# Index score products of the sparse attention tied to the gate tiles of the merge, which move up in the fill

## The reference, cut to what matters

```
r, k, v, wd, ad, g = split(pa)                  # RWKV: 8 heads of 64, state scanned over time
q, k, v, gate, iq, ik, iw = split(pb)           # DSA: 8 heads; iq has 8 index heads of 64, ik one
# per block of 128 queries:
sc = einsum('bqhd,bsd->bqhs', iq, ik) * 64**-0.5
idx_score = einsum('bqhs,bqh->bqs', relu(sc), iw)     # masked by chunk
sel = top_k(idx_score, 128)                            # keys each query may see
p = softmax(q.k over sel) ; y_b = p.v * sigmoid(gate)
# merge with two gates of 1024 columns each
merged = sigmoid(gm[:, :1024]) * (y_a @ w_a_out) + sigmoid(gm[:, 1024:]) * (y_b @ w_b_out)
x = x + ada_gate * (merged @ w_o)
```

## Time and profile before

| what | value |
|---|---|
| median of three runs | 3110.51 us |
| the profiled execution, its own time | 3113.39 us |
| its span, first to last instruction | 3111.6 us |
| TensorE busy | 2990.5 us, 96% |
| VectorE busy | 1606.2 us, 52% |
| mean granted TensorE clock | 0.983 |

### The profile page before, as it was taken

How to read it: one execution, slowest core, us unless ns; L and a number is a source line. 1 busy time by engine, 2 the same in 40 slices (tenths; PEclk the granted TensorE clock), 3 DMA queues, 4 the chain that set the end, 5 groups by cost and what they waited for, 6 DMA issues and landing times.

```text
span 3111.6 us, 42487 instructions
## 1 busy us (share of the span) xinstructions
PE 2990.5 (96%) x16912; PEld 2391.9 (77%) x16912; DVE 1606.2 (52%) x3295; ACT 1079.1 (35%) x1781; POOL 1412.3 (45%) x1817
## 2 busy tenths in 40 slices
PE   6998999999999999999999999999899999999999
PEld 5777777777888877767777678888776778788887
DVE  5776567565666317569744443331366773433310
ACT  4443333333322224233234333222255553332221
POOL 4554344344556544314334255555443334655554
PEclk9999999999999999989999989999999999999999
DMA  3211111112344322001112112223321112222232
GB/s 128 74 63 55 62 55 67 57 52 85 123 147 144 122 88 72 29 33 63 35 55 75 62 61 95 95 97 98 98 80 56 59 61 84 83 94 96 95 102 88
DMA packets 72358, 248.02 MB, mean 80 GB/s; under 512 B 8160, under 2 KB 8544, under 8 KB 72032
## 3 DMA queue, kind: packets, MB, share of 16 engines
q1 hardware_dynamic: 72160, 245.30, 23.4%
HBM read 243.18 MB, written 2.10 MB: 79 GB/s over the span
## 4 chain that ended last, share of the span: by engine, by line
PE 84%; DVE 12%; ACT 2%; issue 1%; POOL 1%; DMA 0%; SPq 0%; DVEq 0%; ACTq 0%; POOLq 0%
PE bank L1054 23%; PE bank L1056 22%; PE bank L1055 22%; PE bank L1102 3%; PE bank L1088 3%; PE bank L1533 1%; PE bank L1551 1%; PE bank L1065 1%; DVE sm L1617 1%; PE bank L1542 1%; DVE sm L1619 1%; DVE t L1764 1%; PE bank L1372 1%; DVE sm L1621 1%; POOL t L2943 1%
## 5 line engine op out<-in xcount | busy, mean ns | idle before, releaser
L2910 POOL TENSOR_TENSOR R<-W,R 128x256 fp32r<-128x256 f32 x1715 | 1286.9, 783 | 1560.9 <-ACT R L2518 1560.8
L1054 PE MATMUL bank<-u,R 128*128 128x512 f32 (+1 forms) x3440 | 1392.3, 405 | 30.9 <-DVE t L1764 7.7
L1056 PE MATMUL bank<-u,R 128*128 128x512 f32 (+1 forms) x3440 | 1349.0, 392 | 0.0
L1055 PE MATMUL bank<-u,R 128*128 128x512 f32 (+1 forms) x3440 | 1347.6, 392 | 0.0
L1054 PEld LDWEIGHTS bank<-u,R 128*128 128x128 f32 (+1 forms) x3440 | 649.3, 189 | 188.7 <-issue 15.8
L1056 PEld LDWEIGHTS bank<-u,R 128*128 128x128 f32 (+1 forms) x3440 | 648.2, 188 | 142.2 <-issue 0.6
L1055 PEld LDWEIGHTS bank<-u,R 128*128 128x128 f32 (+1 forms) x3440 | 650.4, 189 | 127.3 <-issue 4.3
L2518 ACT ACTIVATE R<-W 128x1024 fp32r<-128x1024 f32 (+2 forms) x454 | 452.3, 1002 | 160.8 <-PE bank L1056 154.1
L2548 ACT ACTIVATE u<-t 128x512 fp32r<-128x512 f32 x126 | 78.5, 630 | 326.7 <-DVE t L1742 250.1
L1753 DVE SCALAR_TENSOR_TENSOR X<-bank,X 128x512 f32<-128x512 f32 x32 | 22.1, 692 | 260.2 <-PE bank L1056 260.2
L1720 DVE TENSOR_TENSOR u<-t,u 128x512 fp32r<-128x512 f32 x126 | 99.0, 796 | 101.1 <-ACT u L2548 100.4
(11 more groups left out here) (389 smaller groups left out, 2766.2 us busy)
## 6 DMA issues: line engine op xcount, KB each, us to landing
W<-in_in SPq DMA_DIRECT2D x48, 512.0 KB, 3.3
W<-in_ff_in SPq DMA_DIRECT2D x44, 512.0 KB, 3.2
W<-in_g_qkv SPq DMA_DIRECT2D x24, 512.0 KB, 3.2
W<-in_ada SPq DMA_DIRECT2D x24, 512.0 KB, 3.3
W<-in_f1g SPq DMA_DIRECT2D x22, 512.0 KB, 3.2
W<-in_f1u SPq DMA_DIRECT2D x22, 512.0 KB, 3.2
W<-in_f2g SPq DMA_DIRECT2D x22, 512.0 KB, 3.2
W<-in_f2u SPq DMA_DIRECT2D x22, 512.0 KB, 3.2
```

Source lines behind the costliest of these rows:

```text
L1054: e.matmul(b[0:cols, :], wh, hi, start=(k == 0), stop=False)
L1055: e.matmul(b[0:cols, :], wh, lo, start=False, stop=False)
L1056: i = e.matmul(b[0:cols, :], wl, hi, start=False, stop=(k == KT - 1))
L2910: i = e.tensor_tensor(R[q % NH][:, 1024 + a:1024 + b], W[p % NW][:, a:b], R[q % NH][:, a:b].bitcast(F32), SUB)
```

## The change

`gm` 0 to 7 move from the head of `rest` into `first`, between `iw` and `pa` 2. Each score product gets one more thing that the planner makes it wait for: product n may open only after the last piece of gate tile n // 3 is placed. No instruction is added or taken away, and no wait on the chip is written by hand; the static order of each engine, and with it the order of the panels' transfers, is what changes.

```
-    "ixw": lambda: [("ixp", "iw", 0)], "ixs": lambda qb, h: [("ixp", "iq", 3), ("ixw",)],
+    "ixw": lambda: [("ixp", "iw", 0)], "ixs": lambda qb, h: [("ixp", "iq", 3), ("ixw",), opens("gm", IXN(qb, h) // 3)],
...
-    rest = [s for j in range(8) for s in tiles("gm", j, ("gate", "gm", j, M2[j]))] + gates
+    rest = gates
...
-    first += tiles("iw", 0, ("ixp", "iw", 0)) + pa(2, 6, 10, 3, 7, 11)
+    first += tiles("iw", 0, ("ixp", "iw", 0)) + [s for j in range(8) for s in tiles("gm", j, ("gate", "gm", j, M2[j]))]
+    first += pa(2, 6, 10, 3, 7, 11)
```

## The result

| | median us | runs | range |
|---|---|---|---|
| before | 3110.63 | 4 | 3109.94 to 3112.45 |
| changed | 3149.22 | 4 | 3148.01 to 3156.38 |

The ratio is 1.012, 95% interval 1.0098 to 1.0141: the change costs 38.6 us between the medians, where 3109 was forecast and 3123 was the top of the range. The profiled execution took 3149.84 us for a span of 3148.1, 36.5 more than the span before. All lines of the changed kernel stand one further down (L1054 is L1055).

A forecast was written before the change was run, and what follows sets the result against it. TensorE's own work was taken to bound the kernel, with chains of small VectorE steps bounding the preparation of pairs 2 and 3. The terms summed to -1.5 us on a median of 3110.5, giving 3109 us, range 3099 to 3123.

The forecast's parts named there:

- run, clock behind it, groups, moved tiles: Up to `ru(2)`: product run -4.5 us, full clock behind it -1.5, six product groups +3.0, six gate tiles moved ahead +33.1 and +0.4.
- `ru(3)` to `r2p(3)`: First stretch, preparation of pairs 2 and 3: same fill, fewer top-k rounds, -2 us (0 to -4).
- inversions and `rm`: Second and third stretches, losing dense fill and top-k rounds: -13.5 us (-16 to -8) and -3.9 us (-0.5 to -6).
- nine pieces out of the scan, at the full clock: Scan of pairs 2 and 3: each dense piece taken out gives 1.51 us, nine of them -13.6 us (-13 to -14).
- clock in pairs 2 and 3: In the scan of pairs 2 and 3, idle time can lower the clock further than now: +1 us (0 to +3).
- stages behind: Attention and merge after the scan: no change expected; over 3 us either way would mean the mechanism is wrong.
- Rival 3: Among the gate tiles: product groups lower the clock, granted clock under 0.9, sum +11.1 us, 3122 us; chance 0.05.
- the place of the top-k: Top-k rounds, 56.6 us in all, start before the moved tiles and are mostly over before pair 3's preparation.
- no run of more than three products: Sign of being right: behind the scan of pairs 0 and 1, products come in groups of three, clock near 1.00.
- some 19 us shorter: Sign of being right: the stretch from `r2p` of pair 3 to the first scan step shortens by about this.
- Rival 1: Pairs 2 and 3 bound by latency: inversions and `rm` gain only 8.0 and 1.5 us, 3119 us; chance 0.27.
- Rival 2: Pairs 2 and 3: VectorE was crowded by top-k, 3.3 us wait in pair 3's preparation goes, 3102 us; chance 0.28.

The follow-up runs named there:

- e1: The changed kernel plus 24 unread matmuls of 512 columns ahead of the first scan step of pairs 2 and 3: 3126.6 us.
- e6: The changed kernel with e1's burst of 24 matmuls and twelve of every sixteen top-k rounds left out: 3112.4 us.
- e9: The changed kernel with the top-k rounds of query blocks 2 and 3 put behind the scan of pairs 2 and 3: 3142.7 us.
- e3: The changed kernel with the top-k rounds as a planner chain of their own, no longer behind the products: 3149.1 us.
- e8: The kernel before, its own fill lists kept, with product n tied to gate tile n // 6: 3112.8 us.
- e12: The kernel before with e8's looser tie and the top-k rounds of query blocks 2 and 3 put behind the scan: 3119.2 us.
- e7: The changed kernel with gate tiles 10 and 11 held back for the scan of pairs 2 and 3: 3141.5 us.
- e2: The changed kernel plus two unread 512-column matmuls ahead of each of the 16 scan half steps of pairs 2 and 3: 3167.5 us.

## Why the prediction was wrong

Terms as the prediction has them, against the profiled executions:

| step | forecast us | measured us |
|---|---|---|
| to `ru(2)`: run, clock behind it, groups, moved tiles | -4.5 - 1.5 + 3.0 + 33.5 = +30.5 | +32.0 |
| `ru(2)` to `ru(3)` | no term | +10.2 |
| `ru(3)` to `r2p(3)` | -2.0 | -5.3 |
| inversions and `rm` | -13.5 - 3.9 = -17.4 | -13.9 |
| nine pieces out of the scan, at the full clock | -13.6 | -13.3 (e1) |
| clock in pairs 2 and 3 | +1.0 | +23.7 (scan alone, e1) |
| stages behind | 0 | -0.1 |

**The step that failed is "Idle time there can lower the clock further than now: +1 us (0 to +3)".** The -13.6 beside it was right for a scan at 2.4 GHz: e1's scan of 37.1 us is 13.3 below the 50.35 of before. But the term took the full clock for given in a scan that had just been emptied of its wide matmuls. The earlier trace rows hold the one half step without a piece from which I priced it, and it came right behind a half step with one. The scan is then 60.8 us, 23.7 more than in e1, and this turned -12.6 into +10.5. Rival 3 looked for a low clock in the groups; there it is 1.00 in both windows of the groups. It was the right mechanism at the wrong place. I priced only what idle time does to the clock while it lasts, and not that small matmuls may fail to bring the clock back: the low stretch has 60.31 busy us in 60.80. The Trainium skill (TensorE: Matmul & The Clock Gate, section What's actually happening) lets the clock follow how busy TensorE has been; by that rule the scan would have had its full clock, and here the row on which it was busy throughout, as the profile counts it, at 0.52 decides against it.

**The second step that failed is the place of the top-k: "they can start after product 7, before the moved tiles, with VectorE nearly free for some 30 us more".** VectorE was free, for 20.3 us of idle, but the rounds didn't go there. Products and rounds are one chain (`ix + top`), and the planner looks only a few steps ahead in it, so rounds follow products; tied products hold them back, and the first round is 29 us later than before. They were not "mostly over before pair 3's preparation": of L2162 alone 9.0 us lie between `ru(3)` and the scan. From `ru(2)` to the scan the forecast was -19.4 us and the measured sum is -9.0: 10.4 us are missing, beside 1.5 in the first row. The rows of the table inside this stretch must not be read one by one, since the fill stood elsewhere than I had it ("same fill" for the first stretch is wrong). Of the +10.2 between `ru(2)` and `ru(3)` some 5.5 are 24 dense matmuls more, at 0.23 each; of the -5.3 behind it some 2.8 are 12 fewer; the sum over the stretch has the 90 fewer that I reckoned with. That crowding by rounds is what took the 10.4 is shown by size: fewer rounds ahead of the scan make this same stretch 11.0 us shorter (e6 against e1) or 13.5 (e9 against the changed kernel). e3 shows that earlier rounds don't help by themselves.

**What held, and what held by luck.** The moved tiles are not free ahead of `pa` 2: `ru(2)` starts 32.0 us later against 30.5. Stages behind are untouched. No dense piece is left from the inversions to the end of the scan. The groups are cheap, with waits of 0.94, 0.25 and 0.23 us in all, but they are four and not the six that were priced, and "no run of more than three products" did not come true; that the row still comes out near is partly luck. Of the forecast's own signs, "some 19 us shorter" from `r2p` of pair 3 to the scan does not fit its sum, which gives 17.4; 13.9 were measured. **Rival 1** (bare latency) would have shortened the stretches from `r2p(3)` by under 10 us; they lost 13.9 even with the rounds in them. Its sign was over 8 us of new idle time before L1102 and L1421; between `r2p(3)` and the scan there are 6.4 us of such idle time against 1.3 before (8.5 with that before L1088). And e9's whole way ran at the full clock with TensorE busy for 110.56 of 116.06. **Rival 2** falls: the wait of 3.3 us is still 2.8, and VectorE is fuller than before.

## What to carry to other kernels

The dense tiles beside this chain of small matmuls did two jobs: they filled, and they held TensorE's clock or brought it back. Before moving such tiles away, price the emptied chain at half clock too: here a half step with a piece cost 3.94 us, without one 2.43 or 4.06. Look also at how the emptied chain is entered: behind idle time of 1.7 us it ran at 0.52 (changed kernel), right behind dense matmuls at 1.00 (e1), 0.87 (e8) or 0.54 (e6). And ask of every order that a planner writes where the work behind the moved step in the same chain goes, since free time on an engine is not used by what is not offered.

## What the hardware showed unexpectedly

Small matmuls of 64 and 128 columns, back to back, kept 2.4 GHz for 37 us once they had it (e1). In the changed kernel they did not regain it in the 57 us that were left of the scan, though TensorE was busy all the time; in e8 the same kind of matmuls, again alone, lost it for some 10 us and then had it back for the last 19. Behind the same 24 matmuls of 512 columns e1's profile shows the full clock to the scan's end and e6's a fall after 4 us, with the same instructions on TensorE: a burst doesn't settle it. That it raises the odds is argued from the times: seven of e6's ten lie at 3110.6 to 3116.5 us. Other scans fall too, in places where the changed kernel's profile has 1.00. Windows of the scan of pairs 0 and 1 in e1, then in e12; both begin where only score products stand between the small steps, and in e1 the full clock is back with the second dense piece (from 1359.2):

```profile
1340.00:1360.00 20.00, 20.00 (x103) 14.66 (x102) 6.71 (x23) 3.84 (x10) 2.80 (x4) 0.57 0.07 26
```
```profile
1340.00:1380.00 40.00, 40.00 (x196) 28.97 (x196) 14.11 (x48) 9.09 (x21) 2.79 (x4) 0.58 0.04 14
```

In e6 such a fall accounts for most of an execution's excess, 19.3 of 22.4 us. That it also makes the upper group of times of the kernel before is argued from the sizes, not shown: no profile of that kernel with a fall in its scans was taken. What decides in a scan stays open too. The changed kernel and e9 have both idle time of about 1.6 us at the entry and no wide matmuls behind it, and fell for good; e7 has the idle time and wide matmuls behind it, fell, and was back within 4 us; e1, e6 and e8 enter behind wide matmuls and have none in the scan, and one held, one fell for good and one fell and came back. Two wide matmuls in each half step restored nothing (e2).
